# Taking the unread TensorE products out of the norms and the delta heads of a two-block decoder kernel

## The reference

```python
def _rms_norm(x, gain):
    xf = x.astype(jnp.float32)
    y = xf * lax.rsqrt(jnp.mean(xf * xf, axis=-1, keepdims=True) + EPS)
    return (y * gain.astype(jnp.float32)).astype(x.dtype)

def _modulated_norm(h, gain, shift, scale):
    return _rms_norm(h, gain) * (1.0 + scale) + shift

# first block, per layer: norm -> swiglu -> norm -> mixer (layer 0 gated delta rule,
# layer 1 window attention) -> norm -> swiglu, each added to x (and to ctx)
# second block:
    u = rms_norm(h, norm_mix[i])
    proj = u @ w_in[i]
    ...
    h = h + merged @ w_mix_out[i]
    h = h + memory_cross_attention(rms_norm(h, norm_xattn[i]), ...)
    u = rms_norm(h, norm_mlp[i])
    h = h + jnp.square(jax.nn.relu(u @ w_mlp_up[i])) @ w_mlp_down[i]
```

## Time and profile before

| | |
|---|---|
| runs | 2954.56, 2959.94, 2963.52 us |
| median | 2959.94 us |
| profiled execution | 2956.96 us |
| its span, first to last instruction | 2955.0 us |
| mean granted TensorE clock in it | 0.981 |
| busy, share of the span | PE 95%, PEld 82%, DVE 52%, ACT 40%, POOL 52% |

### The profile page before, as it was taken

How to read it: one execution, slowest core, us unless ns; L and a number is a source line. 1 busy time by engine, 2 the same in 40 slices (tenths; PEclk the granted TensorE clock), 3 DMA queues, 4 the chain that set the end, 5 groups by cost and what they waited for, 6 DMA issues and landing times.

```text
span 2955.0 us, 52281 instructions
## 1 busy us (share of the span) xinstructions
PE 2811.4 (95%) x21638; PEld 2427.7 (82%) x21638; DVE 1540.9 (52%) x2922; ACT 1186.2 (40%) x2076; POOL 1543.2 (52%) x861
## 2 busy tenths in 40 slices
PE   7999999988889999999999998999998998998999
PEld 5888878877777788887888885799997898997999
DVE  4777235535554667316665136554284865723570
ACT  4222234324453322223222244544445465544553
POOL 4444453343324544444444452388884565696697
PEclk9999999999999999999999998999998999999999
DMA  6555322210001555324554225155553343354365
GB/s 256 203 198 200 99 76 82 89 58 3 4 3 51 174 176 178 128 93 144 178 182 156 93 89 100 57 195 190 173 186 101 109 142 108 108 164 136 116 199 164
DMA packets 106123, 381.05 MB, mean 129 GB/s; under 512 B 11392, under 2 KB 16800, under 8 KB 104608
## 3 DMA queue, kind: packets, MB, share of 16 engines
q1 hardware_dynamic: 87456, 310.60, 32.2%
q10 hardware_dynamic: 18432, 67.12, 6.5%
HBM read 373.47 MB, written 4.19 MB: 128 GB/s over the span
## 4 chain that ended last, share of the span: by engine, by line
PE 82%; DVE 8%; POOL 3%; ACT 3%; issue 2%; DMA 1%; SPq 0%; ACTq 0%; DVEq 0%
PE bank L231 23%; PE bank L232 22%; PE bank L233 22%; POOL weights_lo L224 2%; PE bank L822 2%; DVE norm_work L504 1%; PE upper_banks L1555 1%; DVE norm_work L498 1%; PE upper_banks L231 1%; PE upper_banks L232 1%; PE upper_banks L233 1%; DMA ada_first<-w_ada 1%; DVE square_sums L451 1%; PE bank L919 1%; PE upper_banks L838 1%
## 5 line engine op out<-in xcount | busy, mean ns | idle before, releaser
L224 POOL TENSOR_TENSOR weights_lo<-weights_landing,weights_hi 128x1024 fp32r<-128x1024 f32 x554 | 1338.5, 2423 | 1101.0 <-ACT weights_hi L214 1100.4
L214 ACT ACTIVATE weights_hi<-weights_landing 128x1024 fp32r<-128x1024 f32 x554 | 586.5, 1061 | 1235.2 <-PE bank L233 1112.7
L231 PE MATMUL bank<-normed_hi,weights_lo 128*128 128x512 f32 (+1 forms) x2664 | 912.2, 342 | 17.6 <-POOL normed_lo L520 11.9
L232 PE MATMUL bank<-normed_lo,weights_hi 128*128 128x512 f32 (+1 forms) x2664 | 900.9, 338 | 0.0
L233 PE MATMUL bank<-normed_hi,weights_hi 128*128 128x512 f32 (+1 forms) x2664 | 900.0, 338 | 0.0
L231 PEld LDWEIGHTS bank<-normed_hi,weights_lo 128*128 128x128 f32 x2664 | 502.3, 189 | 95.2 <-POOL normed_lo L520 27.6
L233 PEld LDWEIGHTS bank<-normed_hi,weights_hi 128*128 128x128 f32 x2664 | 502.1, 188 | 61.6
L232 PEld LDWEIGHTS bank<-normed_lo,weights_hi 128*128 128x128 f32 x2664 | 502.6, 189 | 58.4
L231 PE MATMUL bank<-hidden_hi,weights_lo 128*128 128x512 f32 (+1 forms) x960 | 329.1, 343 | 0.0
L232 PE MATMUL bank<-hidden_lo,weights_hi 128*128 128x512 f32 (+1 forms) x960 | 329.1, 343 | 0.0
L233 PE MATMUL bank<-hidden_hi,weights_hi 128*128 128x512 f32 (+1 forms) x960 | 329.1, 343 | 0.0
(11 more groups left out here) (447 smaller groups left out, 3912.1 us busy)
## 6 DMA issues: line engine op xcount, KB each, us to landing
weights_landing<-w_up SPq DMA_DIRECT2D x176, 512.0 KB, 3.5
ada_rows<-w_ada_rows ACTq DMA_DIRECT2D x128, 512.0 KB, 4.3
weights_landing<-w_down SPq DMA_DIRECT2D x88, 512.0 KB, 3.4
weights_landing<-w_dn SPq DMA_DIRECT2D x33, 512.0 KB, 3.4
weights_landing<-w_mlp_up SPq DMA_DIRECT2D x32, 512.0 KB, 3.4
weights_landing<-w_mlp_down SPq DMA_DIRECT2D x32, 512.0 KB, 3.5
weights_landing<-w_gate SPq DMA_DIRECT2D x24, 512.0 KB, 3.4
weights_landing<-w_xbc SPq DMA_DIRECT2D x24, 512.0 KB, 3.5
```

The costliest lines, as they stand in the source:

```text
L214: k.nc.scalar.activation(k.WH[:, u % SLOTS, :], k.W[:, u % LANDS, :], ACT.Copy).then_inc(*k.AC.mark(("unit hi", u)))
L224: k.nc.gpsimd.tensor_tensor(k.WL[:, u % SLOTS, :], k.W[:, u % LANDS, :], k.WH[:, u % SLOTS, :].bitcast(F32), ALU.subtract).then_inc(*k.PO. ...
L231: nc.tensor.matmul(out, ll, rh, start=start, stop=False, skip_group_check=True)
L232: nc.tensor.matmul(out, lh, rl, start=False, stop=False, skip_group_check=True)
```

## The change

It removes `busy_pe` and all its calls: in the norms the call in `sums_pe`, the one ahead of the spread's wait and the 7 or 4 behind the spread, with the two tables that chose them; in the delta heads the 4 and the 7 calls ahead of head 0 and the one call in each later head's sixth level, together with the wait for `vnew` that stood ahead of it (the products of line 949, queued before on TensorE, wait for the same `vnew` themselves). Nothing else is changed and nothing is moved.

```diff
--- before.py
+++ after.py
@@ -414,12 +414,6 @@
     mm.then_inc(*k.PE.mark((st, "stat", d)))
 
 
-def busy_pe(k, n, bank=6):
-
-    for _ in range(n):
-        k.nc.tensor.matmul(k.B[bank][:, 0:256], k.C["ident"], k.C["cond_pack"][:, 0:256], start=True, stop=True)
-
-
 def sums_pe(k, pe, st, tokens):
 
 
@@ -428,8 +422,6 @@
         for c in range(tokens // P):
             mm = k.nc.tensor.matmul(ck(k.B[4], c), ck(src, c), k.C["ones"],
                                     start=not last and c == 0, stop=last == 1, skip_group_check=True)
-        if not last and st not in QUIET:
-            busy_pe(k, 1)
     mm.then_inc(*k.PE.mark((st, "stat", KT - 1)))
 
 
@@ -458,21 +450,11 @@
     k.nc.scalar.activation(k.rms[:, 0:n], sums, ACT.Sqrt, scale=1.0 / D, bias=k.C["eps"]).then_inc(*k.AC.mark((st, "rms")))
 
 
-QUIET = ("norm00", "norm xattn")
-
-
 def spread_pe(k, pe, st, tokens, bank=5):
-    if st not in QUIET:
-        busy_pe(k, 1)
     pe.wait_ge(*k.DV.after(st, "r"))
     for c in range(tokens // P):
         mm = k.nc.tensor.transpose(k.B[bank][:, c * P:(c + 1) * P], k.rr[:, c:c + 1].to_broadcast([P, P]), k.C["ident"])
     mm.then_inc(*k.PE.mark((st, "spread")))
-    if st not in QUIET:
-        busy_pe(k, BUSY[tokens])
-
-
-BUSY = {TOK: 7, LAT: 4}
 
 
 def norm_act(k, act, st, work, hi, parts, when=None):
@@ -886,9 +868,6 @@
     else:
         r, q = quadrant(d)
         pe.wait_ge(*k.DV.after("head", i, "xt", d))
-        if i and d == 0:
-            pe.wait_ge(*k.DV.after("head", i - 1, "vnew", 3, 0))
-            busy_pe(k, 1, 2)
         pe.wait_ge(*k.DV.after("head", i, "y", s - 1, d))
         four_last(k, k.B[d], q, lambda c: k.at_[p][d][r, c, q], lambda c: k.xt[r, c, :], ("head", i, "p", s, d))
 
@@ -969,9 +948,7 @@
 def heads_pe(k, pe):
     head_kv_pe(k, pe, 0)
     head_decay_pe(k, pe, 0)
-    busy_pe(k, 4, 2)
     head_kq_pe(k, pe, 0)
-    busy_pe(k, 7, 2)
     for i in range(DN_HEADS + 1):
         levels, after = i < DN_HEADS, i + 1 < DN_HEADS
         for s in range(1, LAST + 1):
```

## The result

| | before | after |
|---|---|---|
| median | 2959.51 us (2954.56 to 2963.52) | 2976.1 us (2975.4 to 2979.64) |
| ratio after / before | | 1.0059, 95% interval 1.0042 to 1.0077 |
| profiled execution | 2956.96 us | 2979.64 us |

The change makes the kernel 16.6 us slower. The forecast was 2963.6 us, within a range that ended at 2971: it was wrong. What came is rival A of the prediction, the heads losing the clock, at 2976 instead of 2973. The profiled execution of after is the longest of its four runs, 3.5 us over their median, and that of before is 2.6 us under its own; so the two traces differ by 22.7 us where the medians differ by 16.6.

A forecast was written before the change was run, and what follows sets the result against it. The prediction took TensorE's queue being held up, or its clock being lower, as the bound; its terms 0 + 1.6 + 1.5 + 0 + 0.6 = +3.7 us, on the median 2959.94, gave 2963.6 us, range 2956 to 2971.

The forecast's parts named there:

- rival A: Delta heads: clock falls between vnew and the last level in each of seven heads, some 11 us, giving 2973; chance 0.10.
- the delta heads: Delta heads: calls fill waits, a clock fall would cost about 1 us; +0.6 us for all, bounds 0 and +2.
- The long norms: Norm01, 02, 10, 11: low clock at the ramp's start, lag won back by the eighth block; 0 each, bounds 0 and 2.3.
- Rival B: Norm01, 02, 10, 11 do not catch up: four times 1.5 to 2.3 us, giving 2971; chance 0.08.
- Norm12: In norm12 second sums start 0.6 us earlier, against a ramp at the low clock; net 0, bounds -0.8 and +1.5.
- Norm mix: In norm mix a low-clock stretch in full products loses 1.8 us, 0.21 regained; +1.6 us, bounds 0 and +2.7.
- Norm mlp: In norm mlp the low clock lasts another stretch, in full products; +1.5 us, bounds 0 and +2.7.
- rival D: Elsewhere, such as a window loop: the removal shifts the order, either sign, 5 us or more; chance 0.05.
- Rival C: Norms and heads: no fall, or other waits cover it, and the queue is freed; -0.6 to -3.6 us, 2957 to 2959; chance 0.19.

The follow-up runs named there:

- experiment 1: Kernel before with only the one call in each of heads 1 to 7, and its wait for `vnew`, taken out: 2970.21 us, +11.8 us.
- Experiment 5: Kernel before without the six calls in each of norm12, norm mix and norm mlp: 2959.17 us, +0.9 us.
- Experiment 3: Kernel before with the call in each of heads 1 to 7 exchanged for four 128 x 128 transposes: 2959.17 us, +0.3 us.
- 4: Kernel before without the nine calls in each of norm01, norm02, norm10 and norm11: 2954.14 us, -4.1 us.
- 8: Kernel before without the seven calls behind the spread in norm01, 02, 10 and 11: 2953.3 us, -5.0 us.
- 9: Kernel before without the seven calls behind the spread in norm01 alone: 2954.3 us, -4.4 us.
- 11: Kernel before without the seven calls behind the spread in norm01, 02, 10, 11, and with two calls instead of one in heads 1 to 7: 2957.14 us, ratio 0.9986.
- kernel 2: Kernel after with the one call per head put back in heads 1 to 7: 2960.3 us, +0.6 us against before.
- 12: Kernel before with norm01's seven calls behind the spread kept in number but cut to 32x32 by 32 columns: 2959.59 us, +0.6 us.
- 6: Kernel before without the four and the seven calls ahead of head 0: 2957.42 us, -0.6 us.

## Why the prediction was wrong, point by point

**The step that failed: the delta heads.** I took +0.6 us, with a bound of +2; it is +11.8 by experiment 1 and +16.2 in the trace of after. Two things went wrong in it.

First, *whether it falls*. I granted that the call fills a wait, and then counted the o products, kT and vT as cover enough for the clock. I made windows at norms and at head 0, none at the place of the removed call. There TensorE was busy for 2.68 of 3.20 us in before: one call of it 0.43 us, the o products some 1.4, and the rest 32x32 and 64x64 work. Without the call it was 2.18 of 3.10, and the clock fell in each of heads 1 to 6.

Second, *for how long*. "A fall there would cost about 1 us" took a stretch of 3.4 us. The stretches are 6.8 and 10.2 us. From head 0's to head 6's sixteen products after takes 200.5 us; six heads of 30.4 us are 182.4; the 18.1 us more go with 44.8 us at the low level (50.2 with what hangs over from head 0), 0.36 to 0.40 us for each. The 30.4 us are those of before's later heads; against before's own 186.2 us, its stops among them, it is 14.3 us or 0.32 for each. So the price for one microsecond, two thirds of 0.45 in my sum, was if anything low, and the length was mis-sized by two to three. Experiment 5 shows the other end: stretches of 3.4 us cost 0.2 to 0.4 us each.

**Rival A** had the right place and, by 7 x 3.4 x 0.45, nearly the right sum by luck: it is one head fewer, with stretches two to three times as long. Against it I set and the earlier trace rows, the eight transposes before the clock rose. Experiment 3 confirms that transposes count. But it was an argument on what kind of work holds the clock, where the question was how much work is left in that place.

**The long norms**, 0 each: right, step by step. In norm01 the low level came at the start of the ramp, the products ran without waits, POOL's waits were back before the eighth block, and that one starts 12.41 us after the first product, for 12.39. Over norm02, 10 and 11 the difference between the two traces, 16.2 us, is the same behind each as ahead of it. Rival B is out. What the step did not see is that kernels 4, 8, 9 and 11 gain 4 to 5 us; no row that I read had to do with it, and neither after nor kernel 2 shows it.

**Norm12**, 0: the second sums start 0.84 us after the first instead of 1.58, a gain of 0.74 (0.6 forecast), and the ramp at 0.50 gives back more than that, +0.5 us net in the trace. **Norm mix**, +1.6: the trace has +1.6. **Norm mlp**, +1.5: +0.8. The low level is longer than forecast, 10.2 us, but 5.8 us of it pass before the first product at 2793.55, and of the 2.0 us that the ramp falls back 1.2 are won again by 2823. Together +2.9 us in the trace (3.1 forecast) and +0.9 with an interval of 3 us to either side by experiment 5.

**What the rest adds.** After norm mix the trace of after loses another 2.3 us in the last part of the attention that follows. Windows of after, and of before over the same work, 20 us earlier:

```profile
2327.10:2337.20 10.10, 9.88 (x39) 6.17 (x40) 5.11 (x21) 4.55 (x17) 0.00 (x0) 0.50 0.01 2
```

```profile
2306.00:2316.00 10.00, 7.87 (x51) 5.48 (x52) 6.81 (x30) 4.94 (x19) 0.00 (x0) 1.00 0.01 2
```

No call was removed there. Kernels 4, 5 and 12 lose 2.5 to 2.7 us at this point too (in 5 the low level is from 2309.0 to 2319.2), and 12 differs from before in norm01 alone. It is rival D, at half the size that I gave it, and may go either way from one kernel to the next. Some 1.4 us more no single place shows. Rival C's gain by a freed queue isn't there beyond norm12's 0.7 us; by its own terms its lower end was 2956.3 us, not 2957.

**The chances.** A had 0.10 on the strength of an argument without a window at its own place. The busy share there, with one call taken off it, would have spoken for A; how much more, I can only say afterwards.

## What to carry to other kernels

A product that nobody reads may be worth many times its own time, so its removal is costed from the window it stands in: how much TensorE work is left there, counted without it, and how long a low level lasts in this kernel where it did occur. The price for each place is the length of a stretch times 0.3 to 0.4 us here (0.45 in a full queue), and less where waits can take it up; the number of places multiplies it. And an edit far upstream can move time in a program with hundreds of very short products: when an engine stops with no releaser in the middle of equal instructions, count the instructions between the stops before a difference of some microseconds is put down to the work that was removed. Here four kernels with fewer instructions in norm01 are 4 to 5 us faster than before (8 is the fastest, 2953.3 us), and two others that move the same stops are not.

## What the runs showed of the hardware that I had not expected

- One product of 0.43 us per head, in a wait for DVE, is worth 11.8 us over seven heads. Without it the clock is at 1.2 GHz for 6.8 or 10.2 us in each of heads 1 to 6; with it, not at all after head 0 in the traces of before, 2, 3 and 4, and two to five times in the other kernels with a call in the heads, for 3.4 us each but for one stretch of 10.2 us in 6 and in 8.
- f32 transposes on the whole array hold the clock as products do (2959.17 against 2958.8 us); four 64x64 products in the same place hold it less well (+4.4 us; in the trace of a run of 2967.5 us in three of seven heads).
- Low stretches of 3.4 us in the heads cost 0.2 to 0.4 us each, those of 6.8 to 10.2 us 0.3 to 0.4 us per microsecond.
- In sets of 64 sums of 32x32, 0.75 us each, TensorE stops for 0.3 to 1.7 us with nothing that it waits for, at distances of some 126, 252 or 504 records and at the same record numbers when 14 records, 240 us upstream, are taken out. That kernel is 4.4 us faster, and not so when seven tiny products take their place; that the stops are the reason isn't shown.
